# Two unequal parts of the tokens, and the high and low half of the input moved by one matmul

## The reference

```python
def swiglu(h, w_gate, w_up, w_down):
    return (jax.nn.silu(h @ w_gate) * (h @ w_up)) @ w_down
...
        xp = xp + yp
        xs = xs + ys
        xp = xp + swiglu(rmsnorm(xp, norm_ffn[i]), ffn_w_gate[i], ffn_w_up[i], ffn_w_down[i])
        xs = xs + swiglu(rmsnorm(xs, norm_ffn[i]), ffn_w_gate[i], ffn_w_up[i], ffn_w_down[i])
```

## Time and profile before

| | |
|---|---|
| median of 3 runs | 2045.07 us |
| span of the profiled execution | 2049.0 us (the page gives no other time of that execution) |
| PE busy | 2003.5 us, 16576 matmuls |
| VectorE busy | 1416.2 us |
| ScalarE busy | 1060.2 us |
| POOL busy | 255.0 us |
| mean granted clock of TensorE | 0.992 |
| read from HBM, written | 194.53 MB, 8.60 MB |

### The profile page before, as it was taken

One profiled execution on the slowest core, in us unless ns is written; L12 is line 12 of the kernel. 1 busy time (PEld: TensorE's weight loads), 2 busy tenths in 40 slices (PEclk: granted clock), 3 DMA queues, 4 the chain that ended last, 5 costly groups with the idle time before them and its releaser, 6 DMA issues.

```text
span 2049.0 us, 41542 instructions
## 1 busy us (share of the span) xinstructions
PE 2003.5 (98%) x16576; PEld 1937.9 (95%) x16576; DVE 1416.2 (69%) x2412; ACT 1060.2 (52%) x1842; POOL 255.0 (12%) x253
## 2 busy tenths in 40 slices
PE   8999999999899999999999979999999999999999
PEld 7999999997599999999999859999999989999999
DVE  4994697468768946974466765895597269937952
ACT  5563465365355634653777753563365355624642
POOL 3000000169420000001111124000000120000001
PEclk8999999999999999999999999999999999999999
DMA  6233333244222333333532253233333313333332
GB/s 187 75 104 93 103 103 99 77 134 107 78 66 80 104 93 103 104 98 88 175 109 89 87 210 87 83 95 94 99 110 91 114 53 91 97 93 110 104 98 80
DMA packets 350021, 208.22 MB, mean 102 GB/s; under 512 B 9897, under 2 KB 340553, under 8 KB 349812
## 3 DMA queue, kind: packets, MB, share of 16 engines
q1 hardware_dynamic: 345988, 198.26, 33.4%
q0 software_dynamic: 3472, 6.96, 1.0%
q10 hardware_dynamic: 384, 0.55, 0.1%
HBM read 194.53 MB, written 8.60 MB: 99 GB/s over the span
## 4 chain that ended last, share of the span: by engine, by line
PE 82%; DVE 7%; POOL 4%; ACT 3%; issue 2%; DMA 1%; ACTq 0%; SPq 0%; POOLq 0%; DVEq 0%
PE acc L681 44%; PE pair L881 18%; PE acc L881 9%; PE bank L881 4%; POOL conv L2575 4%; PE pair L1083 1%; PE pair L762 1%; PE bank L1103 1%; DVE xn L1983 1%; DVE w_lo L1842 1%; PE pair L1058 1%; DMA hist_rows<-in_state_pool 1%; DVE w_lo L2019 1%; DVE block L2019 1%; DVE xt L2053 0%
## 5 line engine op out<-in xcount | busy, mean ns | idle before, releaser
L1316 ACT ACTIVATE w_hi<-raw 128x768 fp32r<-128x768 f32 (+1 forms) x220 | 199.3, 906 | 429.9 <-PE acc L681 426.7
L681 PE MATMUL acc<-h_hi,w_hi 128*128 128x260 f32 x1408 | 399.5, 284 | 0.0
L681 PE MATMUL acc<-h_lo,w_hi 128*128 128x260 f32 x1408 | 398.2, 283 | 0.0
L681 PE MATMUL acc<-h_hi,w_lo 128*128 128x260 f32 x1408 | 397.6, 282 | 0.0
L1842 DVE TENSOR_TENSOR w_lo<-raw,w_hi 128x768 fp32r<-128x768 f32 (+1 forms) x220 | 241.8, 1099 | 216.8 <-ACT w_hi L1316 211.4
L681 PE MATMUL acc<-xin_hi,w_hi 128*128 128x260 f32 x1152 | 331.8, 288 | 6.1 <-DVE w_lo L1842 4.9
L681 PE MATMUL acc<-xin_hi,w_lo 128*128 128x260 f32 x1152 | 325.5, 283 | 0.0
L681 PE MATMUL acc<-xin_lo,w_hi 128*128 128x260 f32 x1152 | 324.9, 282 | 0.0
L681 PEld LDWEIGHTS acc<-h_hi,w_hi 128*128 128x128 f32 x1408 | 265.2, 188 | 0.6
L681 PEld LDWEIGHTS acc<-h_hi,w_lo 128*128 128x128 f32 x1408 | 265.0, 188 | 0.0
L681 PEld LDWEIGHTS acc<-h_lo,w_hi 128*128 128x128 f32 x1408 | 264.8, 188 | 0.0
(11 more groups left out here) (441 smaller groups left out, 5301.3 us busy)
## 6 DMA issues: line engine op xcount, KB each, us to landing
raw<-in_ffn_w_gate SPq DMA_DIRECT2D x88, 512.0 KB, 4.0
raw<-in_ffn_w_up SPq DMA_DIRECT2D x88, 512.0 KB, 5.2
raw<-in_ffn_w_down SPq DMA_DIRECT2D x64, 384.0 KB, 3.6
raw<-in_ffn_w_down SPq DMA_DIRECT2D x64, 320.0 KB, 3.3
raw<-in_attn_w_qkv SPq DMA_DIRECT2D x24, 512.0 KB, 3.9
raw<-in_conv_w_in SPq DMA_DIRECT2D x16, 512.0 KB, 4.1
raw<-in_conv_w_out SPq DMA_DIRECT2D x8, 512.0 KB, 4.4
in_mix<-in_cache_k SPq DMA_DIRECT2D x8, 512.0 KB, 5.3
```

The costliest lines, as they stand in the source:

```text
L681: last = pe.matmul(acc[:, b, 0:HALF], w[:, w_tile * P:(w_tile + 1) * P], v[:, h * HALF:(h + 1) * HALF], start=start and t == 0, stop=stop ...
L1316: act.activation(w_hi[n.slot(2)][:, 0:cols], raw[:, q.slot(4), 0:cols], ACT.Copy).then_inc(split_hi, 1)
```

## The change

The tokens are divided 282 + 238 instead of 260 + 260. The first part lies in the last 282 columns of its bank, the second in the first 238 of the next, so that the 520 sums of a tile are contiguous in PSUM over the border of the banks.

- In tiles added to x, the second part's w_hi k_hi and w_hi k_lo become one matmul: the moving operand is both parts of the input, two runs of 238 columns, and the result is 476 columns wide, k_hi's product in the first 238 and k_lo's in the next. w_lo k_hi is added to the first 238 as before. A contraction step has five matmuls.
- VectorE then adds the extra 238 columns to x (`add_extra`, with a semaphore `folded` that the second add waits for), and then the 520 sums.
- In all other tiles (and in the first tile of conv_out) the three products stay apart: six matmuls, three of 282 and three of 238 columns.
- High and low part of an input lie in one tensor (xin, h_both, mix_both).

```diff
+BANK = 512
+FIRST = 282
+REST = T - FIRST
...
+        h_both = take("h_both", [P, 2, FH, T], F32R)
+        h_hi, h_lo = h_both[:, 0], h_both[:, 1]
...
-            def half_products(m, h, w_tile, s, k_hi, k_lo, start, stop):
-
-                b = 2 * m.slot(2) + h
-                for t, (w, v) in enumerate(((w_hi[s], k_hi), (w_hi[s], k_lo), (w_lo[s], k_hi))):
-                    last = pe.matmul(acc[:, b, 0:HALF], w[:, w_tile * P:(w_tile + 1) * P],
-                                     v[:, h * HALF:(h + 1) * HALF],
-                                     start=start and t == 0, stop=stop and t == 2)
-                return last
...
+            def first_part(m, w_tile, s, both, start, stop):
+
+                to = acc[:, 2 * m.slot(2), BANK - FIRST:BANK]
+                w = slice(w_tile * P, (w_tile + 1) * P)
+                pe.matmul(to, w_hi[s][:, w], both[:, 0, 0:FIRST], start=start, stop=False)
+                pe.matmul(to, w_hi[s][:, w], both[:, 1, 0:FIRST], start=False, stop=False)
+                return pe.matmul(to, w_lo[s][:, w], both[:, 0, 0:FIRST], start=False, stop=stop)
+
+            def second_part(m, w_tile, s, both, start, stop):
+
+                to = acc[:, 2 * m.slot(2) + 1, 0:2 * REST]
+                w = slice(w_tile * P, (w_tile + 1) * P)
+                pe.matmul(to.rearrange("p (x c) -> p x c", x=2), w_hi[s][:, w], both[:, :, FIRST:T], start=start, stop=False)
+                return pe.matmul(to[:, 0:REST], w_lo[s][:, w], both[:, 0, FIRST:T], start=False, stop=stop)
+
+            def second_part_apart(m, w_tile, s, both, start, stop):
+
+                to = acc[:, 2 * m.slot(2) + 1, 0:REST]
+                w = slice(w_tile * P, (w_tile + 1) * P)
+                pe.matmul(to, w_hi[s][:, w], both[:, 0, FIRST:T], start=start, stop=False)
+                pe.matmul(to, w_hi[s][:, w], both[:, 1, FIRST:T], start=False, stop=False)
+                return pe.matmul(to, w_lo[s][:, w], both[:, 0, FIRST:T], start=False, stop=stop)
...
+            def add_extra(m, to):
+
+                dve.tensor_tensor(to[:, FIRST:T], extra_of(m), to[:, FIRST:T], ALU.add).then_inc(folded, 1)
+                dve.wait_ge(folded, At(folds_to(m.start), m.step, m.i).v)
...
-                        dve.tensor_tensor(halves(x[:, c, :]), accumulator(At(c)), halves(x[:, c, :]), ALU.add).then_inc(evacuated, 1)
+                        add_extra(At(m0 + DOWN_M[0] + c), x[:, c, :])
+                        dve.tensor_tensor(x[:, c, :], accumulator(At(c)), x[:, c, :], ALU.add).then_inc(evacuated, 1)
```

More of the change, by code:

```diff
@@ L101, in key_takes, with folds_to @@
     return n // 3 + 1 if n % 3 == 2 else 2 * (n // 3) + n % 3 + 1
+ONE_PIECE = {TILE[f"ffn{layer}"] + j for layer in range(4) for j in range(2 * PLAIN)}
+ONE_PIECE |= {TILE["conv_in"] + j for j in range(2 * KT)} | {TILE["qkv"] + j for j in range(3 * HEADS)} | {TILE["conv_out"]}
+def folds_to(m):
+    return sum(1 for t in range(m + 1) if t not in ONE_PIECE)
 class At:
@@ L686, in tile_products, with part_of @@
[L686 to L692, removed]
+            PARTS = (slice(0, FIRST), slice(FIRST, T))
+            def part_of(h):
+                return acc[:, 0, BANK - FIRST:BANK] if h == 0 else acc[:, 1, 0:REST]
+            def first_part(m, w_tile, s, both, start, stop):
[4 more added lines that the diff above has]
+                return pe.matmul(to, w_lo[s][:, w], both[:, 0, 0:FIRST], start=False, stop=stop)
@@ L694, in unit, with tile_products @@
+            def tile_products(m, w_tile, s, both, start, stop, second=second_part):
+                first_part(m, w_tile, s, both, start, stop)
+                return second(m, w_tile, s, both, start, stop)
+            def unit(n, m, both, k0=0, k1=KT, kn_=KT, before=None, second=second_part):
                 pe.wait_ge(split_lo, (n + 1).v)
@@ L699, in unit @@
                         before(k)
-                    last = tile_products(m, k - k0, n.slot(2), hi[:, k, :], lo[:, k, :], k == 0, k == kn_ - 1)
+                    last = tile_products(m, k - k0, n.slot(2), both[:, :, k, :], k == 0, k == kn_ - 1, second)
                 last.then_inc(units_done, 1)
@@ L717, in before @@
                         means(r)
-                unit(n, m, xin_hi, xin_lo, before=before)
+                unit(n, m, xin, before=before, second=second_part_apart)
                 if r in (1, 7):
@@ L869, in ffn @@
                 for j in range(1, 2 * PLAIN):
[L870 removed]
+                    unit(At(u + j), At(m0 + j), xin, second=second_part_apart)
                 def block(J, b):
```

65 lines of the change are left out of this document (36 added, 29 removed).

## The result

The changed kernel takes **2060.75 us** (median of 4 runs, 2060.27 to 2060.94) against 2044.77 (4 runs, 2042.2 to 2051.78): ratio 1.0071, interval 1.0050 to 1.0092. It is slower by 0.7%; forecast was 2018.4 with a range of 2004 to 2042.

What follows compares the result with a forecast made beforehand. PE was taken as the bound, fp32r matmuls held at 120.3 ns by the weight load. Terms -34.1 + 4.3 + 2.5 + 0.6 = -26.7 us took the median 2045.07 to 2018.4; 8-in-10 range 2004 to 2042.

Steps and rivals of the forecast that it cites:

- The floor of the weight load: Joined tiles: weight load holds fp32r matmuls at 120.3 ns; one load fewer saves 39.8 ns a step, 34.1 us.
- rival 2: All fp32r matmuls: stream slower than one column a cycle at full clock, 0.463 ns a column; 2057.6 us, chance 0.07.
- weak place: The forecast's floor: the 6 ns between the 114 measured for a weight load and the assumed 120 stay unexplained.
- A rule against it: Trainium skill's rule: load 107 ns, matmul N/2.4 + 2.5, so 260 columns are column-bound at 110.8 ns; +2 and +9 us.
- Tiles not joined: Three matmuls of 282 and three of 238 columns, all under the floor: 0 us; bound 16.3 us more gained.
- allowance of 1 ns: Each 282-column matmul, joined tiles or not, may end past the floor by 1 ns: 4.3 us in all.
- Two runs: Joined matmul's moving operand of 476 columns, two runs of 238 from two places: costs 0.
- VectorE inside a tile: Extra add of 238 columns in each joined tile, 0.43 to 0.48 us, hidden behind PE's matmuls.
- Ends of stages: Extra adds exposed where x ends a stage: four ends at 0.4 us, two direct waits at 0.45; 2.5 us.
- The pooling tiles: Extra adds in the 16 pool tiles, counted as exposed only in the upper bound of 9 us.

Runs made afterwards that it cites:

- e9: Kernel before with matmul rows behind its end, other engines idle: fp32r with 32 weight columns (512: 231.6 ns, 128: 60.0), then whole contraction steps (264 + 256 joined: 719.5).
- e1: Kernel before with rows of 24 matmuls behind its last one, by width, type and weight columns: fp32r 111.7 ns at 64 columns, 119.9 at 260, 229.3 at 512.
- e3: Changed kernel, joined, without the added VectorE adds (output incomplete): 2056.32 us, ratio 1.0034 to the kernel before.
- e6: Changed kernel with the pooling tiles multiplied apart and without their added adds: 2053.4 us, ratio 1.0032 to the kernel before.
- e2: Changed kernel with all products apart (282 + 238 columns, nothing joined) and no added adds: 2059.3 us, ratio 1.0056 to the kernel before.

## Why the prediction was wrong

**The floor of the weight load, -34.1 us: failed, and the rest hangs on it.** The step that failed is the inference from the earlier trace rows: "A fixed amount added to each matmul would still be there; something that runs beside the columns and ends last only at the full clock would not." The row is right, and a fixed amount is excluded, as e9 confirms. But a stream that takes 0.46 ns a column at the full clock and the array's 0.83 at half clock passes that test too. It was written down as rival 2, with the remark that it "too would vanish at half clock", and got 0.07. And the forecast's own floor does not pass: it took the load as a time that stays while the clock halves, and no row showed a load at half clock. e1 does. Its clock fell to 0.50 in the row of 128 columns and stayed there for that of 192 (the second line is four starts of it; one lasts 0.415 us):

```profile
2054.30:2059.40 5.10, 5.10 (x25) 5.10 (x25) 0.00 (x0) 0.00 (x0) 0.00 (x0) 0.50 0.00 0
```

```profile
2055.62 1.05 PE L1306 MATMUL acc<-h_hi,w_hi 128*128 128x192 f32 x4
```

(1.05 - 0.415) / 3 = 0.212 us from start to start, 213 ns over the row, and as much for the last matmuls of 128 columns, though 192 columns at 1.2 GHz are 160 ns. So the load of 128 weight columns takes 213 ns at half clock, nearly twice the 112 of the full one. A floor of 120.3 grown by the same factor would be some 229 ns (an estimate), and the earlier trace rows have 215.7. The row that was taken as the ground for the floor speaks against it. What spoke against the slower stream was plain fp32, two records of 216.7 ns at the same bytes; e1 has that again (219.3), and it does not decide, since that form takes two cycles a column and may hide a slower stream. What spoke against the floor was in the text as its weak place: the earlier trace rows gave 114 ns for a load, not 120, and the 6 ns between had no cause. The 6 ns above its own measurement belonged to the columns. Joined steps went from 721.4 to 722.6 ns (63.48 and 63.59 us over 88 steps), 856 x 1.2 = +1.0 us.

**Rival 2 gave the size.** It had 130.5, 220.2 and 114 ns; measured 130.9, 219.0 and 110.3. Joined +3.3 us forecast, +1.0 found; apart +6.7 forecast, 576 x (729.6 - 718.7) = +6.3 found. Its total, 2057.6, is 3.2 below the result, and that nearness is in part luck: it has the joined steps 2.3 us too dear and leaves out the 6.2 us of the pooling stages. Nor do all the 6.3 us apart reach the end: the stages of these tiles grew by 3.5 (gate/up 2.7, attention with qkv 1.1, conv_in -0.3). The mechanism: joining saves no columns, only a load that was already hidden beside 260 of them, and the division puts matmuls of 238 columns, three in a step apart and one in a joined step, below the 112 ns floor. 238 columns at 0.46 would take 109; the floor takes 112. The estimate in the prediction's passage "A rule against it", +2 and +9 us, has the same mechanism, columns above a floor of the load, with 110.8 ns for 260 columns where 119.9 were measured; it was set aside for the size and had the sign right.

**Tiles not joined, 0 us (a gain to 16.3 on one side): wrong in sign.** The matmuls of 238 columns did fall from 120 to 112 ns, the gain that stood as a bound, but those of 282 columns went to 131 ns; the allowance of 1 ns for them was some 10 short.

**Two runs, 0 us: nearly right.** 216.7 against 213.7 ns for 476 columns (e1), 3 ns or less.

**VectorE inside a tile, hidden: right.** e3 against after, 63.60 us both. In the timeline of a tile's end, where the earlier trace rows were, the low part of the weights starts 1.16 us after the first add, 0.5 later than before, and PE does not wait:

```profile
934.48 0.41 DVE L1887 TENSOR_TENSOR x<-acc,x 128x238 f32 x1 [1.91 <-PE acc L708]
935.02 0.70 DVE L2188 TENSOR_TENSOR x<-acc,x 128x520 f32 x1
935.64 0.82 DVE L1873 TENSOR_TENSOR w_lo<-raw,w_hi 128x640 fp32r<-128x640 f32 x1
```

**Ends of stages, 2.5 us: right where directly waited for (0.45 us each), too much elsewhere.** At the four ends behind POOL's adds 0.4 us each were forecast; PE's waits for the sum there come to 0.3 us in all, in two of them (none in e3). PE's two direct waits, ahead of the second pooling layer and at the program's end:

```profile
1655.71 1.30 PE L768 MATMUL pair<-avg,sqacc 128*128 128x2 f32 x8 [1.43 <-DVE sqacc L2194]
...
2054.97 0.66 PE L968 MATMUL bank<-const,x_out 128*128 128x128 f32 x4 [1.23 <-DVE x_out L2188]
```

1.43 for the 0.99 of the earlier trace rows, 1.23 for the 0.79 of the earlier trace rows: +0.44 each.

**The pooling tiles, in the 2.5 us only as an upper bound of 9: mis-sized.** VectorE's room was read in the down half and carried to tiles with a fifth of the products. There the stages grew by 6.2 us, and with the adds left out by 0.1 or less (both of e6, the second of e3; its first has 1.4 us of half clock, as the kernel before has the earlier trace rows). The term belonged in the sum.

**The share of each part.** By stages of the traces: pooling 6.2 of 12.4, steps apart and below the floor 3 to 6, the rest small. By the runs: division alone +11.7 (e2), joining with the adds left out +8.7 (e3), pooling tiles put back -8 to -11 (e6). These don't add up to better than some 4 us: one kernel's runs spread over 13 us (2042.44 to 2055.87), the first product of the first pooling stage starts between 24.4 and 31.7 us, and half-clock stretches of 3.4 us or more come in some executions and not in others. By the traces, the start left out, the stages of e2 come to +9.2 us, those of e3 to +5.4 (1.4 of it half clock in its first pooling stage), those of the changed kernel to +11.8.

## What to carry to other kernels

Before a saving is built on "the time of one instruction is X, its work is Y, so X - Y is overhead", measure the same instruction at two or three widths: rows of 24 matmuls at 128, 260 and 512 columns would have shown 112, 120 and 229 ns, a floor that 260 columns lie above, and ended the forecast. Two mechanisms that vanish in the same test are not told apart by it, and a time that is said to stay while the clock halves has to be seen at both clocks. And read the room of an engine in each stage to which work is added, the shortest tiles first, not in the stage that has the most time.

## What the runs showed of the hardware

At the full clock fp32r matmuls start every 0.45 to 0.47 ns a column (e1, e9; 231.6 ns for 512), bf16 ones of 512 columns every 215.9 ns (e1). The Trainium skill (TensorE: Matmul & The Clock Gate, "Back-to-back issue gap") gives, for the gap of single matmuls at the full clock, N/2.4 + 2.5 ns. e1's bf16 row agrees (56.3, 110.8, 215.9 for 55.8, 110.8, 215.8 by the rule); the fp32r row doesn't, and there the measurement decides: by the rule with N = 282 and 476, 120.0 and 200.8 would stand where 131.1 and 213.7 were measured.

The load of 128 weight columns holds an fp32r matmul at 112 ns at the full clock (64 to 238 columns) and at 213 ns at half clock (192 columns, e1). 32 weight columns let one of 128 columns start every 60 ns. In bf16 one of 128 columns starts every 56.3 ns with all 128 weight columns, so the floor of 112 ns is not there for that type.

Why fp32r is slower by 7%, why 476 columns take 213.7 ns in one row and 219 to 220 in the kernels (after, e3) and in e9's row with 32 weight columns, and why the joined step of 264 + 256 is 5 ns shorter in the kernel than in a row of its own, the runs do not say.
